# A slab's matmuls over 512 tokens for all input tiles and then over the other 256, in a two-layer diffusion trunk on one core

## What is computed

```
def conv_ffn(h, w_up, conv_w, conv_b, w_down):
    u = h @ w_up                                   # 1024 -> 2 * 2816
    ...
    gate, val = jnp.split(acc, 2, axis=-1)
    return (jax.nn.silu(gate) * val) @ w_down      # 2816 -> 1024

# layer 0 (latent and context tokens): p = h @ w_in ; y = heads @ w_out ; h = layer_norm(2 ** 0.5 * h + g1 * y)
# then h = layer_norm(2 ** 0.5 * h + g2 * conv_ffn(h * (1 + sc2) + sh2, ...))
# layer 1: GLA projections of both token groups; its output projection and its FFN are of latent tokens only
```

## Time and profile before

| what | value |
|---|---|
| time, median of 3 runs | 1986.97 us (1980.5 to 1989.19) |
| span of the profiled execution | 1984.4 us |
| PE busy | 1777.4 us (90%) |
| PEld busy | 1528.6 us (77%) |
| DVE busy | 1289.2 us (65%) |
| ACT and POOL busy | 703.1 and 700.8 us (35% each) |

### The profile page before, as it was taken

How to read it: one execution, slowest core, us unless ns; L and a number is a source line. 1 busy time by engine, 2 the same in 40 slices (tenths; PEclk the granted TensorE clock), 3 DMA queues, 4 the chain that set the end, 5 groups by cost and what they waited for, 6 DMA issues and landing times.

```text
span 1984.4 us, 26373 instructions
## 1 busy us (share of the span) xinstructions
PE 1777.4 (90%) x9560; PEld 1528.6 (77%) x9560; DVE 1289.2 (65%) x1749; ACT 703.1 (35%) x997; POOL 700.8 (35%) x402
## 2 busy tenths in 40 slices
PE   6999878996999999999999889987777899999996
PEld 5888767785788888888887768867666677887875
DVE  7687688679988678864554652138783566365455
ACT  1211334422443223322334552334342445243344
POOL 1354776347556555553002300018672210000002
PEclk9899989997899999999999789998888899999997
DMA  7222111122223333232212011210001223232321
GB/s 313 75 85 106 59 43 43 64 75 85 78 100 119 127 127 120 101 119 95 64 63 77 32 33 53 74 61 1 1 1 53 75 74 95 88 99 90 99 91 64
DMA packets 37277, 159.92 MB, mean 81 GB/s; under 512 B 4144, under 2 KB 4400, under 8 KB 31056
## 3 DMA queue, kind: packets, MB, share of 16 engines
q1 hardware_dynamic: 37200, 158.89, 23.2%
HBM read 156.78 MB, written 2.10 MB: 80 GB/s over the span
## 4 chain that ended last, share of the span: by engine, by line
PE 74%; DVE 15%; issue 4%; ACT 3%; POOL 3%; DMA 0%; DVEq 0%; ACTq 0%; POOLq 0%; SPq 0%
PE pm L388 57%; PE pm L408 4%; DVE ada_sum L1162 2%; DVE probs L1309 2%; PE pm L564 2%; PE pm L688 1%; PE pm L530 1%; PE pm L370 1%; DVE fade L1548 1%; PE pm L554 1%; PE pm L706 1%; DVE pairs L1609 1%; PE pm L420 1%; PE pm L432 1%; DVE h_res L1338 1%
## 5 line engine op out<-in xcount | busy, mean ns | idle before, releaser
L1137 DVE TENSOR_TENSOR w_lo<-raw,w_hi 128x1024 fp32r<-128x1024 f32 x193 | 276.1, 1431 | 439.6 <-ACT w_hi L799 439.2
L388 PE MATMUL pm<-x_hi,w_hi 128*128 128x512 f32 x1600 | 476.3, 357 | 12.1 <-DVE acc_g L1462 9.1
L388 PE MATMUL pm<-x_lo,w_hi 128*128 128x512 f32 x1600 | 472.1, 355 | 0.0
L388 PE MATMUL pm<-x_hi,w_lo 128*128 128x512 f32 x1600 | 472.0, 354 | 0.0
L799 ACT ACTIVATE w_hi<-raw 128x1024 fp32r<-128x1024 f32 x191 | 202.2, 1059 | 672.1 <-PE pm L388 635.8
L388 PEld LDWEIGHTS pm<-x_hi,w_hi 128*128 128x128 f32 x1600 | 263.1, 191 | 58.5 <-issue 13.0
L388 PEld LDWEIGHTS pm<-x_hi,w_lo 128*128 128x128 f32 x1600 | 262.8, 191 | 43.3
L388 PEld LDWEIGHTS pm<-x_lo,w_hi 128*128 128x128 f32 x1600 | 262.9, 191 | 43.2
L1653 POOL TENSOR_TENSOR ada_w<-ada_w,cond 128x2048 f32<-128x2048 f32 x47 | 186.0, 3957 | 282.7 <-DVE ada_sum L1162 236.1
L1690 POOL TENSOR_TENSOR sum<-sum,sq_t 128x768 f32<-128x768 f32 (+1 forms) x32 | 54.3, 1696 | 561.2 <-ACT sq_t L896 560.7
L388 PE MATMUL pm<-hid_hi,w_hi 128*128 128x512 f32 (+1 forms) x528 | 161.2, 359 | 13.3 <-DVE hid_lo L1471 13.2
(11 more groups left out here) (193 smaller groups left out, 2775.6 us busy)
## 6 DMA issues: line engine op xcount, KB each, us to landing
raw<-slabs SPq DMA_DIRECT2D x193, 512.0 KB, 3.6
ada_w<-ada SPq DMA_DIRECT2D x48, 1024.0 KB, 4.9
h_res<-x SPq DMA_DIRECT2D x4, 768.0 KB, 15.6
out<-h_res SPq DMA_DIRECT2D x8, 256.0 KB, 2.0
level_f<-level SPq DMA_DIRECT2D x1, 896.0 KB, 5.0
rope<-rope SPq DMA_DIRECT2D x1, 512.0 KB, 23.8
vec<-vec SPq DMA_DIRECT2D x1, 272.5 KB, 2.9
band<-band SPq DMA_DIRECT2D x1, 192.0 KB, 3.4
```

Of the source, the lines that this page charges most:

```text
L388: last = pe.matmul(out_p[:, a:b], w[slot][:, ks], x[:, k, a:b], start=(k == 0 and w is w_hi and x is hi), stop=(k == tiles - 1 and w is w_lo))
L1137: dve.tensor_tensor(w_lo[nxt % 2][:, :], raw[nxt % 4][:, :], w_hi[nxt % 2][:, :].bitcast(FP32), ALU.subtract).then_inc(sem["split_lo"], 1)
```

## The change

In `slab` the loop over the two token ranges moves from the inside to the outside. The weights, operands, sums and number of instructions stay as they are. The waits for `ready` are made in the first of the two passes only. Slabs over 512 tokens have one range and come out as before.

```
                     pe.wait_ge(sem["psum_free"], s - 1)
-                for k in range(tiles):
-                    if ready is not None:
-                        pe.wait_ge(ready, value + k + 1)
-                    ks = slice(k * P, (k + 1) * P)
-                    for w, x in ((w_hi, hi), (w_hi, lo), (w_lo, hi)):
-                        for a, b in HALVES if tokens == TOK else HALVES[:1]:
+                for a, b in HALVES if tokens == TOK else HALVES[:1]:
+                    for k in range(tiles):
+                        if ready is not None and a == 0:
+                            pe.wait_ge(ready, value + k + 1)
+                        ks = slice(k * P, (k + 1) * P)
+                        for w, x in ((w_hi, hi), (w_hi, lo), (w_lo, hi)):
                             last = pe.matmul(out_p[:, a:b], w[slot][:, ks], x[:, k, a:b],
                                              start=(k == 0 and w is w_hi and x is hi),
                                              stop=(k == tiles - 1 and w is w_lo))
```

## The result

Four runs of the changed kernel gave a median of 1996.84 us (1995.58 to 1999.05), four of the kernel before 1986.08 us. The ratio is 1.0058, with a 95% interval of 1.0038 to 1.0079: slower by 10.8 us, where +6.6 us was forecast (1993.6 us, in a range of 1977 to 2011). The prediction called anything within 0.5% no change and gave that a chance of 0.58; the 0.58% measured lies just beyond, on the slower side, with an interval (0.38% to 0.79%) that reaches over that border. The profiled execution has a span of 1992.8 us, 8.4 us more than before.

A forecast was written before the change was run, and what follows sets the result against it. PE was taken as the bound in layer 0's FFN and GLA's value slabs. Pace -3.3, first down slabs +6.8 and clock +3.1 gave +6.6 us on 1984.4, 1991.0; with 2.6 for the median, 1993.6 us, range 1977 to 2011.

The forecast's parts named there:

- The first down slabs: Layer 0's three first down slabs: 256s moved behind the last tile's wait add 2.51, 2.51 and 1.79 us, sum +6.8 us.
- The clock: Behind the three longer stops: the clock falls at the two where it did not before, 1.53 us each, +3.1 us.
- The pace: 1662 pairs in up, down and value slabs: a pair goes from 349 to 347 ns, -3.3 us.
- (a): Rival, faster: runs of 256s go at 112 ns or less, -16.6 us by pace, total 1980 us; chance 0.16.
- (b): Rival, slower: weight loads bound runs of 256s, from 122 ns on; 2011 us at 130; chance 0.29, shared with (d).
- (c): Rival, no change: pace stays 122 ns and the three slabs' delay is taken back, 1987 or 1984 us; chance 0.08.
- (d): Rival: clock falls more often or longer, 1.53 us per stretch, 1998 us with three more; chance within 0.47 and 0.29.

The follow-up runs named there:

- e6: Changed kernel plus idle filler matmuls ahead of the last tile's wait, only in layer 0's three waiting down slabs; 1990.41 us, ratio 1.0032 to the kernel before.
- e1: Changed kernel with the old order put back in the first and fifth down slabs of layer 0's groups; 1983.36 us, ratio 0.9984 to the kernel before.
- e2: Kernel before with the new order only in the first and fifth down slabs of layer 0's groups; 1999.0 us, ratio 1.0054 to the kernel before.
- e3: Kernel before, but layer 0's first and fifth down slabs per group run the 256s first, then the 512s; 2002.1 us, ratio 1.009 to the kernel before.
- a0: The changed kernel run again with no further edit; 1996.52 us, ratio 1.0051 to the kernel before.
- e5: Kernel before, but in all six FFN groups' first down slab PE takes the next down slab's first three tiles while waiting; 1964.79 us, ratio 0.9905, repeated 0.9907.
- e7: e5 with the new order in all other slabs; 1968.04 us, ratio 0.9913 to the kernel before.
- e4: Changed kernel plus idle filler matmuls ahead of the last tile's wait, in layer 0's first and fifth down slabs per group; 1999.5 us, ratio 1.0067 to the kernel before.

## Why the prediction was right, and where it was not

**The first down slabs: right.** The prediction had +2.51, +2.51 and +1.79 us there. By e6, with the clock out of the way, the stretch behind the first arrival is +2.35 us and behind the second +2.37 us (12.02 against the 9.65 of the same stretch at full clock). From the third arrival to L432 it is +1.12 us (52.62, 1043.07 to 1095.69, against 51.50, 1040.87 to 1092.37). That these are less than forecast comes from the old order, not from the new: its slabs behind a stop run at a slower pace, which the new order doesn't have (below). The one such slab in the first stretch gives back 0.15 us and the seven short ones of the third group 0.6 us; e1, with the new order in those seven only, takes 50.94 us there (1038.27 to 1089.21). The idle times were forecast as 4.35, 5.28 and 4.70 us and are 4.03, 4.50 and 4.52 us; the records count a matmul as busy for 0.39 us, which is some 0.16 us more than its step, and the second tile came 0.50 us sooner. e1 and e2 show the place, and e3 shows the quantity that counts: the work behind the last wait.

**The clock: right in kind, near in size.** The forecast had it fall at all three stops, for +3.1 us, and it did. In the changed kernel's trace it is 1.52 us behind the first, and 2.06 us behind the second, where it had already cost 1.52 us; behind the third it is 1.33 us, as the arrival of the last tile to L432 takes 53.95 us (1048.34 to 1102.29) and in e6 52.62 (1043.07 to 1095.69). So 3.4 us were added by the change, where 3.1 were forecast. The prediction's reason was that a longer stop brings the fall, and the clock did fall at each of the changed kernel's stops; but between shorter ones the length alone does not decide: the stop of 2.75 us before the change had none behind it, and the second stop of e1, 2.01 us, had one. It is also the part that differs between executions of one kernel: in a second profile of the changed kernel (a0) the first stop lasted longer (6.64 us, below), and the clock was at 0.50 for 6.83 us there, not 3.41.

**The pace: the step that failed.** "So a pair takes 349 ns", and with it "the pair's rest is 122 ns" and the gain of 3.3 us. The 16.75 us from which 349 came holds, beside 48 pairs, the first matmul's slow start and the drawn-out record of the last. Read from start to start most slabs of the kernel before are at 347 ns. Timeline of PE before the change, the second pair of a block and the first of its second slab (23 pairs apart, 7.98 us):

```profile
592.41 0.59 PE L388 MATMUL pm<-x_hi,w_hi 128*128 128x512 f32 x2
592.85 0.51 PE L388 MATMUL pm<-x_lo,w_hi 128*128 128x512 f32 x2
...
600.83 0.50 PE L388 MATMUL pm<-x_hi,w_hi 128*128 128x512 f32 x2
```

And after it, the end of a run of 256s, the run of 512s behind it, and the middle of the next run of 256s:

```profile
566.39 0.28 PE L388 MATMUL pm<-x_hi,w_lo 128*128 128x256 f32 x1
566.51 0.40 PE L388 MATMUL pm<-x_hi,w_hi 128*128 128x512 f32 x1
...
567.67 0.39 PE L388 MATMUL pm<-x_hi,w_lo 128*128 128x512 f32 x1
...
569.93 0.39 PE L388 MATMUL pm<-x_hi,w_hi 128*128 128x512 f32 x1
```

```profile
572.09 0.28 PE L388 MATMUL pm<-x_lo,w_hi 128*128 128x256 f32 x1
...
573.29 0.28 PE L388 MATMUL pm<-x_hi,w_lo 128*128 128x256 f32 x1
```

Ten 256s start in 1.20 us, 120 ns each, as forecast; the ten 512s from 567.67 to 569.93 take 226 ns each. That makes 346 to 347 ns a pair, no less than before. The first five 512s behind a run of 256s take 232 ns each (566.51 to 567.67), which is why two slabs are at 16.80 us and not at 16.75.

The old order has a second pace, which the prediction and its rows mixed with the first. Behind a stop a pair takes 353 ns, in the first group's down slabs for three slabs, in the third's for all seven. The starts of the third and the fourth down slab, before the change and then in e5, which has the same order and no stop:

```profile
664.61 0.48 PE L388 MATMUL pm<-hid_hi,w_hi 128*128 128x512 f32 x1
...
673.17 0.40 PE L388 MATMUL pm<-hid_hi,w_hi 128*128 128x512 f32 x1
```

```profile
662.97 0.59 PE L388 MATMUL pm<-hid_hi,w_hi 128*128 128x512 f32 x2
...
671.38 0.51 PE L388 MATMUL pm<-hid_hi,w_hi 128*128 128x512 f32 x2
```

From start to start the slab takes 8.56 us behind a stop and 8.41 without one; in the new order it is 8.44 us in the same place (669.41 to 677.85). Why a stop sets the slower pace no run here shows. So the change costs 0.02 to 0.03 us in a slab at the fast pace and wins 0.10 to 0.15 us in one at the slow pace. In layer 0's FFN that is +0.6 us in the up slabs and -1.2 us in the down slabs behind the first ones, -0.6 us together where some -3 us were forecast (GLA's eight value slabs are not in this count). With this the three down stages come out: 6.8 + 3.4 - 1.2 - 0.5 (the second tile's earlier arrival) = 8.5 us, beside the 8.7 measured.

That the run of 256s came out at the forecast 120 ns is in part luck: the step of 120 was read at 540.14 to 540.62, in a slab at the slow pace (0.36 us from 512 to 512); at the fast pace a 256's step is 112 to 118 ns. Had the pair been read as 347 ns, the pace term would have been nothing and the sum 6.8 + 3.1 = 9.9 us; the measured difference is 10.8 us, and the ratio's interval is 7.5 to 15.7 us.

**The rivals.** (a), a gain by the pace: the runs of 256s are at 120 ns, not 112, and e7 lies with e5; e1, at 0.9984 (0.9966 to 1.0003), leaves no room for (a)'s 16.6 us. The 109 ns that the Trainium skill gives for matmuls over 256 columns ("TensorE: Matmul & The Clock Gate", "Back-to-back issue gap") is not reached in any run here. (b), loads as the bound: with nothing but 256s in a row the step is 120 ns, so the slower pace that it needs (130 to 174 ns) did not come. Its threshold of 122 ns was no threshold, since it was set against a pair that is 347 and not 349. (c), the delay taken back: the down stages grew by 8.7 us and the span by 8.4, so it reached the end. (d), further falls of the clock: the low stretch at the second stop doubled, which cost 0.54 us more than before and not 1.53.

## What to carry to other kernels

Ahead of a loop change ask of each wait inside the loop what work stands behind its last firing, not only whether the wait is still met: here 21 matmuls (15 in the third group) that had run inside a wait of 8 to 10 us moved behind it, three times, and that and the clock behind the longer stops were the effect. Where one operand arrives last, put all other work ahead of it, that of the next output tile too; e5 gained 18 us by that without making any instruction faster. Read a pace from start to start inside a block, never from a block's length divided by its count, and in more than one block: 2 ns in 349, times 1662, was the prediction's wrong term, and a second pace stood in the same trace.

## What the runs showed of the hardware

- Runs of fp32r matmuls over 256 columns, each with its own weight load, start every 120 ns at a granted clock of 1.00; alternating with 512s they start 347 ns a pair, and the sum of the two runs (120 and 227) is the same. Behind a run of 256s the first five 512s are slower, 232 ns each.
- The same alternating matmuls have two paces at a granted clock of 1.00: 347 ns a pair, or 353 ns in the slabs behind a stop, for three to seven slabs (8.56 us a slab before the change, 8.41 in e5, which has no stop). In runs of one width the same slabs of the changed kernel show one pace only, 8.44 us.
- Idle matmuls into unused accumulator columns kept the clock at 1.00 at all three stops of e6, whose idle parts were then 2.10, 1.96 and 2.73 us instead of 4.03, 4.50 and 4.52; in e4 they did so at two of three. By the times of whole runs the gain is not clear of noise (e6 is at 1.0032, 1.0016 to 1.0048, the changed kernel at 1.0051 and 1.0058), and by the windows and the third group's times it is 1.52, 2.06 and 1.33 us.
- DVE operations took up to nearly four times as long while POOL was busy. In the trace of the kernel before, `hid_lo` of 768 tokens takes 0.96 us in the nine cases in which POOL stands still and 1.86 to 1.96 us in the thirteen in which it works; the split `w_lo` takes at most 1.23 us in 135 cases without POOL, and all 30 that took over 1.6 us, up to 4.57 us, ran beside a POOL operation. In the second profile of the changed kernel (a0) this held up the first stop: the split of the weights took 4.70 us, not 1.23 as in the same place of the first profile, beside a POOL operation that began in the same moment, and the last tile came 2.6 us later for it (11.69 us after the slab's start instead of 9.08). DVE's and POOL's timelines:

```profile
644.39 4.70 DVE L1137 TENSOR_TENSOR w_lo<-raw,w_hi 128x1024 fp32r<-128x1024 f32 x1
```

```profile
644.39 3.63 POOL L1653 TENSOR_TENSOR ada_w<-ada_w,cond 128x2048 f32<-128x2048 f32 x1 [5.74 <-DVE ada_sum L1162]
```

No run here was made to change one and hold the other; that the two share something is argued from this coincidence, and what they share is not shown.
